# A decoder step on one core: split products in the second half of the first mixer loop, with their lower parts on GpSimd

## The reference, cut to what matters

```python
proj = h @ prm['w_in'][l]
hq, hf, hi, hg, sq, sk, sv, mx, mo, ga, gb, gc = jnp.split(proj, _in_split_points(), axis=-1)
...
pk = past['k'][past['page_table'], l].reshape(B, -1, SB_HEADS, SB_HEAD_DIM)
...
merged = (jax.nn.sigmoid(ga) * (o_a @ prm['w_hg_proj'][l]) + jax.nn.sigmoid(gb) * (o_b @ prm['w_sb_proj'][l])
          + jax.nn.sigmoid(gc) * (o_c @ prm['w_ml_proj'][l]))
```

## Time and profile before

| | |
|---|---|
| runs of the kernel | 1781.12, 1782.02 and 1788.02 us, median 1782.02 |
| span of the profiled execution, first to last instruction | 1779.4 us; its own time isn't given, the fastest run is 1.7 us above its span |
| TensorE busy | 1708.4 us, 96% |
| VectorE, ScalarE, GpSimd busy | 1024.1, 790.2 and 73.4 us |
| mean granted clock of TensorE | 0.983 of full speed |
| the first mixer loop | eight heads of some 61 us, four from 282 us and four from 1160 us |

### The profile page before, as it was taken

How to read it: one execution, slowest core, us unless ns; L and a number is a source line. 1 busy time by engine, 2 the same in 40 slices (tenths; PEclk the granted TensorE clock), 3 DMA queues, 4 the chain that set the end, 5 groups by cost and what they waited for, 6 DMA issues and landing times.

```text
span 1779.4 us, 33104 instructions
## 1 busy us (share of the span) xinstructions
PE 1708.4 (96%) x12604; PEld 1491.2 (84%) x12604; DVE 1024.1 (58%) x1890; ACT 790.2 (44%) x1446; POOL 73.4 (4%) x103
## 2 busy tenths in 40 slices
PE   5999999999999999999989999999999999999997
PEld 3898988878876687999979889788788766979997
DVE  3554545665557666655455554555665765666654
ACT  2554534445333315655345554353454332356652
POOL 0000000000000000000000000000000100000000
PEclk7999999999999999999989999999999999999999
DMA  8678655465556925555647785665464686455551
GB/s 343 251 269 321 226 221 214 171 227 219 200 209 245 328 101 210 186 172 209 258 174 276 292 322 181 230 230 185 165 246 156 238 314 225 156 203 185 180 214 57
DMA packets 85802, 391.81 MB, mean 220 GB/s; under 512 B 12328, under 2 KB 17712, under 8 KB 55344
## 3 DMA queue, kind: packets, MB, share of 16 engines
q1 hardware_dynamic: 72520, 368.15, 56.5%
q10 hardware_dynamic: 13160, 22.02, 3.5%
HBM read 377.30 MB, written 12.83 MB: 219 GB/s over the span
## 4 chain that ended last, share of the span: by engine, by line
PE 82%; DVE 7%; DMA 5%; ACT 2%; SPq 2%; issue 2%; POOL 0%; POOLq 0%; ACTq 0%; DVEq 0%
PE ps L594 18%; PE ps L589 15%; PE ps L590 15%; PE ps L550 13%; PE ps L794 3%; PE ps L793 3%; PE ps L776 2%; PE ps L570 2%; DMA pages<-in_k_pages 2%; PE ps L740 2%; PE ps L658 1%; SPq L446 1%; PE ps L757 1%; PE ps L556 1%; DMA ring<-in_w_ffn_in 1%
## 5 line engine op out<-in xcount | busy, mean ns | idle before, releaser
L1137 DVE TENSOR_TENSOR ring_parts<-ring,pages_parts 128x1024 fp32r<-128x1024 f32 (+1 forms) x288 | 334.0, 1193 | 161.1 <-ACT pages_parts L1761 161.0
L589 PE MATMUL ps<-arena_parts,pages_parts 128*128 128x264 f32 x1536 | 391.2, 289 | 12.8 <-DVE xn_parts L1225 7.6
L1761 ACT ACTIVATE pages_parts<-ring 128x1024 fp32r<-128x1024 f32 (+1 forms) x288 | 285.1, 1028 | 186.0 <-DMA ring<-in_w_ffn_in 56.5
L590 PE MATMUL ps<-xn_parts,pages_parts 128*128 128x264 f32 x1408 | 355.1, 287 | 0.0
L589 PEld LDWEIGHTS ps<-arena_parts,pages_parts 128*128 128x128 f32 x1536 | 293.3, 191 | 30.7 <-issue 28.7
L590 PEld LDWEIGHTS ps<-xn_parts,pages_parts 128*128 128x128 f32 x1408 | 268.2, 190 | 0.0
L594 PE MATMUL ps<-arena_parts,ring_parts 128*128 128x264 f32 x1536 | 227.3, 287 | 0.0
L550 PE MATMUL ps<-xn,ring 128*128 128x264 f32 x896 | 208.9, 389 | 0.5 <-ACT xn L1768 0.5
L594 PEld LDWEIGHTS ps<-arena_parts,ring_parts 128*128 128x128 f32 x1536 | 206.0, 190 | 0.0
L550 PEld LDWEIGHTS ps<-xn,ring 128*128 128x128 f32 x896 | 166.2, 190 | 34.7 <-issue 5.3
L590 PE MATMUL ps<-gates_parts,pages_parts 128*128 128x264 f32 x704 | 176.3, 285 | 0.0
(11 more groups left out here) (353 smaller groups left out, 2489.1 us busy)
## 6 DMA issues: line engine op xcount, KB each, us to landing
ring<-in_w_ffn_in SPq DMA_DIRECT2D x88, 1024.0 KB, 5.3
ring<-in_w_ada SPq DMA_DIRECT2D x32, 1536.0 KB, 6.6
ring<-in_w_a SPq DMA_DIRECT2D x32, 1536.0 KB, 7.2
ring<-in_w_ffn_down SPq DMA_DIRECT2D x32, 1408.0 KB, 6.3
pages<-in_k_pages SPq DMA_DIRECT2D x128, 256.0 KB, 5.7
ring<-in_w_ada SPq DMA_DIRECT2D x24, 1024.0 KB, 6.7
pages<-in_v_pages SPq DMA_DIRECT2D x88, 256.0 KB, 6.3
ring<-in_w_proj SPq DMA_DIRECT2D x8, 1536.0 KB, 9.1
```

Source lines behind the costliest of these rows:

```text
L589: mm(ps[:, b, 0:T], tile, hi[:, k, :], start=start, stop=False)
L590: return mm(ps[:, b, 0:T], tile, lo[:, k, :], start=False, stop=False)
L1137: v.tensor_tensor(ring_lo[:, r, at * P:(at + n) * P], w, whi[:, place, 0:n * P].bitcast(F32), ALU.subtract)\
L1761: A(whi[:, place, 0:n * P], ring[:, r, at * P:(at + n) * P], ACT.Copy).then_inc(S.whi_ready, 1)
```

## The change

In a head's last six products `halved_product` is called with `by_pool`: the upper parts come from ScalarE, which gets the copies between its other steps, and the lower parts from GpSimd (`low_halves`), with a semaphore of their own, `low_half`. TensorE waits for the upper part ahead of a half's upper matmuls and for the lower part between these and the lower ones; the place is given back at the first lower matmul. The first key product moves from behind the gates to behind the scores, the second from behind the level products to behind the fifth of these products, and the transposes of the key scores from behind L894 to the place of the second key product. VectorE copies and scales the key scores ahead of the picks and behind them, and subtracts the next head's first weights at the end. SP loads the pages of a key product right behind the key product before, across heads; after the loop the gate weights have other places and the second of them is loaded behind the last product. GpSimd's loop is written out.

```diff
         p = self.pos
-        return [[(p + j) % SLOTS for j in js] for js in ((0, 1, 0, 3), (1, 0, 2, 3))]
+        return [[(p + j) % SLOTS for j in js] for js in ((1, 0, 1, 3), (0, 1, 2, 3))]
...
@@ -465,21 +465,21 @@
                 for k in range(2):
                     load(ins.w_a[layer, k], 3, at[k])
                 sp.wait_ge(S.yss_ready, 1 + since(S.yss_ready))
+                load_key_pages(0)
                 for i in range(HEADS):
-                    load(ins.w_a[layer, i * 4 + 2], 3, at[2])
-                    load_key_pages(i * 2)
-                    load(ins.w_a[layer, i * 4 + 3], 3, at[3])
+                    for k in range(2, 4):
+                        load(ins.w_a[layer, i * 4 + k], 3, at[k])
+                    load_key_pages(i * 2 + 1)
                     if i < HEADS - 1:
                         for k in range(2):
                             load(ins.w_a[layer, i * 4 + 4 + k], 3, at[k])
-                    load_key_pages(i * 2 + 1)
-                sp.wait_ge(S.tr, HEADS + since(S.tr))
+                        load_key_pages(i * 2 + 2)
                 gate_at, proj_at = slots.mixer_b()
-                for k in range(2):
-                    load(ins.w_b[layer, k], 2, gate_at[k])
+                load(ins.w_b[layer, 0], 2, gate_at[0])
                 for n in (2, 0, 1):
                     load_values(n)
-                for k in (3, 2):
+                sp.wait_ge(slot_done[at[3]], slots.parts[at[3]].n + 1 + since(slot_done[at[3]]))
+                for k in (1, 3, 2):
                     load(ins.w_b[layer, k], 2, gate_at[k])
                 for n in range(3, 16):
                     load_values(n)
...
@@ -600,7 +600,7 @@
                     for at in range(0, depth, PIECE):
                         place, m = pieces.take()
                         ks = range(at, min(at + PIECE, depth))
-                        pe.wait_ge(S.wlo_ready, m + 1 + since(S.wlo_ready))
+                        pe.wait_ge(S.wlo_ready, m + 1 - pooled.n + since(S.wlo_ready))
...
-                def halved_product(r, first):
+                def halved_product(r, first, by_pool=False):
 
                     b, n = products.take()
                     pe.wait_ge(S.evac, n + 1 + since(S.evac))
                     for h in range(2):
                         place, m = pieces.take()
-                        pe.wait_ge(S.wlo_ready, m + 1 + since(S.wlo_ready))
+                        if by_pool:
+                            pe.wait_ge(S.whi_ready, m + 1 + since(S.whi_ready))
+                        else:
+                            pe.wait_ge(S.wlo_ready, m + 1 - pooled.n + since(S.wlo_ready))
                         for k in range(h * HALF, (h + 1) * HALF):
                             tile = hi_halves[place][:, k % HALF * P:(k % HALF + 1) * P]
                             mm(ps[:, b, 0:T], tile, xhi_a[:, k, :], start=(k == 0), stop=False)
                             last = mm(ps[:, b, 0:T], tile, xlo_a[:, k, :], start=False, stop=False)
-                        last.then_inc(S.whi_done, 1)
+                        if by_pool:
+                            pe.wait_ge(S.low_half, pooled() + 1 + since(S.low_half))
+                        else:
+                            last.then_inc(S.whi_done, 1)
                         for k in range(h * HALF, (h + 1) * HALF):
                             last = lower(b, r, first + k, k, xhi_a, k == KC - 1)
+                            if by_pool and k == h * HALF:
+                                last.then_inc(S.whi_done, 1)
                     last.then_inc(slot_done[r], 1)
...
                     last.then_inc(S.zz, 1)
+                    pe.wait_ge(S.qstr, i + 1 + since(S.qstr))
+                    key_pages(0)
                     oslot = open_slot(3, at[2])
-                    product(oslot, 0, xn_of, KC)
-                    product(oslot, KC, xn_of, KC)
+                    halved_product(oslot, 0, True)
+                    halved_product(oslot, KC, True)
...
-                    product(oslot, 2 * KC, xn_of, KC)
+                    halved_product(oslot, 2 * KC, True)
...
                     gslot = open_slot(3, at[3])
-                    product(gslot, 0, xn_of, KC)
+                    halved_product(gslot, 0, True)
                     pe.wait_ge(S.qkv_sb, i + 1 + since(S.qkv_sb))
                     for j in range(3):
                         last = mm(ps[0:8, M1, 0:T], hp[:, WIF + j * 8:WIF + j * 8 + 8], qkv[:, j, i, :],
                                   start=(j == 0), stop=(j == 2))
                     last.then_inc(S.gt, 1)
-                    pe.wait_ge(S.qstr, i + 1 + since(S.qstr))
-                    key_pages(0)
-                    product(gslot, KC, xn_of, KC)
+                    halved_product(gslot, KC, True)
+                    key_pages(1)
...
@@ -880,7 +889,10 @@
                     for t in range(2):
                         last = nc.tensor.transpose(ps[:, M0, t * P:(t + 1) * P], w6[:, t * P:(t + 1) * P], ident)
                     last.then_inc(S.kdtp, 1)
-                    key_pages(1)
+                    pe.wait_ge(S.zrow, i * 2 + 1 + since(S.zrow))
+                    for n in range(4):
+                        last = nc.tensor.transpose(ps[:, Z, n * P:(n + 1) * P], rbuf[:, n * P:(n + 1) * P], ident)
+                    last.then_inc(S.ztr, 1)
                     pe.wait_ge(S.lvc, i * 5 + 5 + since(S.lvc))
                     pe.wait_ge(S.kdtr, i + 1 + since(S.kdtr))
                     sample_rows(M1, pj[:, HI_, TP:T]).then_inc(S.ibr, 1)
...
-                    product(gslot, 2 * KC, xn_of, KC)
+                    halved_product(gslot, 2 * KC, True)
                     pe.wait_ge(S.snr, i + 1 + since(S.snr))
                     for b in range(NB):
                         last = mm(ps[:, M1, b:b + 1], sn8[:, b, :], pj[:, HQ_, TP + b:TP + b + 1],
                                   start=True, stop=True)
                     last.then_inc(S.hos, 1)
-                    pe.wait_ge(S.zrow, i * 2 + 1 + since(S.zrow))
-                    for n in range(4):
-                        last = nc.tensor.transpose(ps[:, Z, n * P:(n + 1) * P], rbuf[:, n * P:(n + 1) * P], ident)
-                    last.then_inc(S.ztr, 1)
...
+                    for _ in range(12):
+                        pieces.take()
...
@@ -1480,6 +1490,9 @@
                     v.tensor_tensor(w6[:, 0:TP], w6[:, 0:TP], w4[:, 0:TP], ALU.mult).then_inc(S.kdr, 1)
 
 
+                    dve.wait_ge(page_free[3], i * 2 + 3 + since(page_free[3]))
+                    v.tensor_copy(rbuf[:], ps[:, Z, :]).then_inc(S.zrow, 1)
...
-                    if i < HEADS - 1:
-                        for n in range(2):
-                            split_halves(at[0], A_ORDER[0][n] * KC)
-
-                    dve.wait_ge(S.ibr, i + 1 + since(S.ibr))
-                    dve.wait_ge(S.klr, i + 1 + since(S.klr))
-                    link(v.tensor_tensor(tt8, ps[:, M1:M1 + 2, :].rearrange("p a (b k) -> p (a b) k", k=P),
-                                         w4[:, TP:T].unsqueeze(2).broadcast_to([P, NB, P]), ALU.mult))
-                    dve.wait_ge(S.snm, i + 1 + since(S.snm))
-                    v.tensor_tensor(sn8[:], sn8[:], tt8, ALU.add).then_inc(S.snr, 1)
-
-                    dve.wait_ge(page_free[3], i * 2 + 3 + since(page_free[3]))
-                    v.tensor_copy(rbuf[:], ps[:, Z, :]).then_inc(S.zrow, 1)
-
...
                     last.then_inc(S.zrow, 1)
+
+                    dve.wait_ge(S.ibr, i + 1 + since(S.ibr))
+                    dve.wait_ge(S.klr, i + 1 + since(S.klr))
+                    link(v.tensor_tensor(tt8, ps[:, M1:M1 + 2, :].rearrange("p a (b k) -> p (a b) k", k=P),
+                                         w4[:, TP:T].unsqueeze(2).broadcast_to([P, NB, P]), ALU.mult))
+                    dve.wait_ge(S.snm, i + 1 + since(S.snm))
+                    v.tensor_tensor(sn8[:], sn8[:], tt8, ALU.add).then_inc(S.snr, 1)
+                    if i < HEADS - 1:
+                        for n in range(2):
+                            split_halves(at[0], A_ORDER[0][n] * KC)
...
                             else:
+                                if n == 2:
+                                    o_slot = ahead.take(3, at[2])
+                                    split_halves(o_slot, 0)
                                 evac(r, before + 2 + n, dests[3 + n])
-                    for k in range(2, 4):
-                        ahead.take(3, at[k])
+                    g_slot = ahead.take(3, at[3])
...
                     softplus_tail(w1, pj[:, HF_, :]).then_inc(S.l1r, 1)
+                    split_halves(o_slot, KC)
...
                     evac(r, before + 2, dests[6])
+                    split_halves(o_slot, 2 * KC)
...
                     A(sgt[:], sgt[:], ACT.Exp, scale=-1.0).then_inc(S.sge, 1)
+                    split_halves(g_slot, 0)
...
+                    split_halves(g_slot, KC)
...
```

(28 more changed lines are left out.)

16 lines of the change are left out of this document (8 added, 8 removed).

## The result

| | before | after |
|---|---|---|
| median of the runs | 1782.07 us (1781.12 to 1788.02, 4 runs) | 1814.18 us (1800.56 to 1821.36, 4 runs) |
| ratio | | 1.017, 95% interval 1.0141 to 1.02 |
| profiled execution, span | 1781.12, 1779.4 | 1821.36, 1819.6 |

The change makes the kernel 1.7% slower. The forecast was 1779.0 with a range of 1766 to 1801: the change went to the side to which 0.24 had been given, and beyond the range. The clock that TensorE was granted in the four executions was 0.972, 0.974, 0.978 and 0.980, in the order 1821.36, 1813.67, 1814.69, 1800.56 us.

What follows compares the result with a forecast made beforehand. TensorE, busy for 96% of 1779.4 us, was taken as the bound. New waits of 41.2 us, less 33.1 for split products and 10.9 for page waits, gave -2.8 and a forecast of 1779 us, range 1766 to 1801.

Steps and rivals of the forecast that it cites:

- the side to which 0.24 had been given: Chance given to a slower kernel, where within 0.5% (1773 to 1791 us) counted as no change.
- The six products: TensorE: six products a head become split ones, 3.61 to 2.92 us each, saving 33.1 us in eight heads.
- The page waits: TensorE's waits for key pages, 10.9 us in eight heads, go through earlier loads.
- The subtraction: GpSimd's subtraction of 128x512 for the lower parts, taken as 1.12 us between rows of other sizes.
- rival C: GpSimd's subtraction is slower, above some 1.25 us; at 1.4, 24 us more, 1803; chance 0.08.
- One hold, 0.8 us: One GpSimd subtraction blocks VectorE for 1.12 less 0.3 us, through the ports they share.
- wait (1): TensorE at the suffix sums: 0.95 us a head from one hold and part of a second, bounds 0 and 2.1.
- Waits (2) to (5): TensorE, a head: attention product 1.3 us, value projection 1.1 more, behind the level products 1.2, sum of squares 0.6 more.
- (3): TensorE at the value projection: the wait grows from 0.27 us by 1.1 more a head.
- (2): TensorE at the attention product: 1.3 us a head, its exponentials standing behind ScalarE's two copies for the fifth product.
- rival D: TensorE's clock falls once a head after waits of about 1 us: 14 us more, 1792; chance 0.08.
- B: Subtractions block VectorE's chain ahead of the suffix sums for their full 1.12 us: 16 more, 1795; chance 0.12.

Runs made afterwards that it cites:

- experiment 6: Kernel before with the first key product and page loads early, and two of the six products split, lower parts on GpSimd: 1759.63 us, ratio 0.9869.
- experiment 1: Changed kernel with GpSimd subtracting only 16 of each half's 512 columns, every instruction and wait kept: 1777.6 us, ratio 0.9976.
- Experiment 8: Changed kernel with ScalarE's two copies for the fifth product moved behind the exponentials of the attention product: 1820.3 us, ratio 1.0216.
- experiment 2: Changed kernel's reordering only (key products, page loads, score transposes, state update), all six products left fp32: 1785.85 us, ratio 1.0023.
- experiment 9: Kernel of experiment 6 with the second product of the third slot split too, its copies ahead of ScalarE's output transfers: 1752.71 us, ratio 0.9839.

## Why the prediction was wrong

By its own steps:

- **The six products**, 6 x 0.69 a head: right (1.46 us for the half of a product in the profile after; 11.5 us for 16 of them in experiment 6 against 11.0).
- **The page waits**, 10.9 us: right, gone in both kernels with early loads.
- **The subtraction**, 1.12 us by interpolation between 0.73 and 1.90: it took 1.265 where nothing met it (two in 2.53 us), and 1.47 in the mean of one group of 48. Near the point of 1.25 that rival C named, but no wait for a lower part stands inside the products.
- **One hold, 0.8 us**: 0.92 to 1.11. The estimate of an overlap of 0.3 at the edges was right for the length (1.265 - 0.3 = 0.97), but stood on the wrong length.
- **How many holds: the step that failed.** "One hold of 0.8 for certain, a part of a second". There were four, in half of the heads five, and wait (1) came to 3.64 us where 0.95 was forecast, 21.5 us more in eight heads. The prediction lists no subtraction with a time, so it does not say which of them it saw in the chain. It missed above all those of the third product: its two copies stand on ScalarE right behind the softplus, their places are freed by then, and GpSimd started at 307.00, just ahead of L1433. The upper bound of 2.1 for wait (1) did not hold all cases either: it should have counted every subtraction whose copy can be ready before 307.5, which is four, 4 x 0.97 less the pause of 0.8 for ScalarE that experiment 1 shows, 3.1, and still without the fifth.
- **Waits (2) to (5)**: forecast 1.3, 1.1 more, 1.2 and 0.6 more a head; measured 1.26, 0.7 more, 1.31 and, in six of eight heads, 0.5 more. The sizes were right but for (3), which was put 0.4 too high. Experiment 8 adds to (2) that the copies do hold the exponentials and are yet worth nothing there.
- **The clock, rival D**, 14 us at a chance of 0.08: 21.6 in the ledger, some 15 by the prices of a fall (18 less the 3.4 of before). It was set up as one fall a head after waits of 1 us. Half of the falls came at waits (1) of 2.5 us and more, half at the sum of squares that ends a head. In experiment 1, where wait (1) is nearly gone, four of the fourteen are left, so most of them follow from it and the rival was not one beside the others. That is the second failure: B and D had been given chances as if they excluded each other. B's 16 us and D's 14 together are 1809, 5 us from the median, but by luck: B has 0.8 us a head of its 16 us in wait (2), which stayed at 1.26, and D has one fall a head where there were nearly two.
- **The chances**: those of B, C and D add up to 0.28, and the forecast's own range ends below 1791, so 0.24 for slower leaves nothing for its upper end.

What was right in the rivals: B named the point from which the lock decides ("more than one GpSimd operation falls into that chain"). Its other half, a hold of the full length, did not come: 0.92 to 1.11 us against a subtraction of 1.265. The Trainium skill, page "SBUF — State Buffer", section "SBUF: two separate sides", states that the pair of ports is an exclusive lock for a whole instruction, against a VectorE operation in a two-port mode or with two SBUF inputs. The rows agree with it: those held are L1424, L1433 and L1436 with two SBUF inputs, L1423 with one (by the page it would have to be in a two-port mode, which no row shows), and the operations that read PSUM were not held (1.14 and 0.69 us in experiment 9). The prediction used the first half of that rule and did not go through the chain link by link with the second.

What stays open: why seven of eight heads have a fall at their end when experiment 2, with a wait of 0.6 us there in every head, has three falls in all, and 2.9 of the 40.2 us of the ledger. The four executions have clocks of 0.972 to 0.980, which fits a varying number of falls, but only one of the four was looked at in rows.

## What to carry to other kernels

An engine that is idle for 96% of the time is not free when it shares a lock: before work is given to GpSimd, write down for each instruction when its input can be ready at the earliest, and which VectorE operation starts then; under a read of PSUM or a pause it costs nothing (11 us won by two products, 6.9 more by a third, put there by moving two copies), in a chain it costs its length less 0.3 us, each time. A hold taken out of one chain goes into the next unless the work stops coming. And a new wait on TensorE has to be priced together with the clock behind it, here 0.9 us more for a fall that the next wait took up in part and 1.6 for one that no wait took up.

## What the runs showed of the hardware

- A VectorE TENSOR_SCALAR with one tensor input and scalars by pointer, 128x264 fp32 in SBUF, is held by a GpSimd subtraction just as one with two inputs: 0.36 to 1.28 us.
- GpSimd's subtraction of 128x512 fp32 with fp32r output takes 1.265 us, of 128x16 0.227; two of 256 columns in a row 1.41.
- The hold goes both ways: two subtractions in VectorE's chain took 3.47 us where two alone take 2.53.
- A fall of the granted clock to 0.50 for 3.4 us made a head 0.9 us longer where the next wait shrank from 1.83 to 1.18 us, and 1.6 us longer where no wait shrank (2.54 and 2.59).
- 22 matmuls whose result nobody reads, put into a wait, kept the granted clock at 1.00 behind it where it had fallen to 0.50. In the first head it fell 6 us later instead.
- VectorE operations with an input in PSUM kept their lengths beside subtractions (128x512 copy 0.69 us, two 128x384 scalings 1.14).
